# A named function table set ahead of the joined mLSTM work, and another spread of the top-k search steps over the phases of a layer

## The reference, cut to what matters

```python
# first block: the keys and queries of the forgetting attention are normalised over each head
q = rms_norm(q, gq) * (Dh ** -0.5);  k = rms_norm(k, gk)
# second kind of layer, one of four mixers (DSA): the best quarter of the keys by an index score
score = jnp.einsum('bqh,bqhs->bqs', wi, relu(q_idx @ k_idx))
score = jnp.where(k_pos <= q_pos, score, NEG_INF)
_, idx = lax.top_k(score, 128)      # then softmax attention over the chosen keys alone
```

## Time and profile before

| | us |
|---|---|
| median of 3 runs (3570.53 to 3570.90) | 3570.84 |
| the profiled execution | 3576.43 |
| its span, first to last instruction | 3574.2 |
| PE busy | 3366.0 (94%) |
| DVE busy | 1521.3 (43%) |
| ACT busy | 1306.0 (37%) |
| mean granted clock of TensorE, of full | 0.962 |

### The profile page before, as it was taken

How to read it: one execution, slowest core, us unless ns; L and a number is a source line. 1 busy time by engine, 2 the same in 40 slices (tenths; PEclk the granted TensorE clock), 3 DMA queues, 4 the chain that set the end, 5 groups by cost and what they waited for, 6 DMA issues and landing times. The chain is left out here.

```text
span 3574.2 us, 37539 instructions
## 1 busy us (share of the span) xinstructions
PE 3366.0 (94%) x14912; PEld 2676.5 (75%) x14912; DVE 1521.3 (43%) x2423; ACT 1306.0 (37%) x2224; POOL 322.1 (9%) x148
## 2 busy tenths in 40 slices
PE   7988789999999999999888999999999998889998
PEld 6755568877888888876676788878887766668886
DVE  4143431125333333344776633343334378663334
ACT  3344542223222323233366423232223335743222
POOL 0411214430000000002200000000000230000000
PEclk9998979999999999999999999999999999999999
DMA  3300213322333333332100233323333210023332
GB/s 133 100 30 24 65 36 105 96 89 84 100 94 100 95 100 95 96 102 83 42 1 24 83 99 96 95 84 99 96 98 104 89 53 7 13 66 100 95 100 71
DMA packets 77069, 280.60 MB, mean 79 GB/s; under 512 B 8800, under 2 KB 9056, under 8 KB 76640
## 3 DMA queue, kind: packets, MB, share of 16 engines
q1 hardware_dynamic: 76896, 278.21, 25.5%
HBM read 276.08 MB, written 2.10 MB: 78 GB/s over the span
## 5 line engine op out<-in xcount | busy, mean ns | idle before, releaser
L521 ACT ACTIVATE w_hi<-raw_slabs 128x1024 fp32r<-128x1024 f32 x496 | 524.3, 1057 | 1321.6 <-PE ps L561 1180.0
L536 DVE TENSOR_TENSOR w_lo<-raw_slabs,w_hi 128x1024 fp32r<-128x1024 f32 x372 | 455.1, 1224 | 748.9 <-ACT w_hi L521 748.8
L561 PE MATMUL ps<-in_hi,w_hi 128*128 128x512 f32 x1904 | 744.6, 391 | 8.3 <-DVE in_lo L878 8.2
L561 PE MATMUL ps<-in_lo,w_hi 128*128 128x512 f32 x1904 | 741.8, 390 | 0.0
L561 PE MATMUL ps<-in_hi,w_lo 128*128 128x512 f32 x1904 | 741.8, 390 | 0.0
L561 PE MATMUL ps<-parts,w_hi 128*128 128x512 f32 x2304 | 713.2, 391 | 7.7 <-PEq L385 7.7
L536 POOL TENSOR_TENSOR w_lo<-raw_slabs,w_hi 128x1024 fp32r<-128x1024 f32 x124 | 306.4, 2473 | 2623.2 <-ACT w_hi L521 2623.2
L561 PEld LDWEIGHTS ps<-parts,w_hi 128*128 128x128 f32 x2304 | 433.7, 188 | 100.0 <-issue 10.0
L561 PE MATMUL ps<-parts,w_lo 128*128 128x512 f32 x1152 | 449.2, 390 | 0.0
L561 PEld LDWEIGHTS ps<-in_hi,w_hi 128*128 128x128 f32 x1904 | 357.9, 188 | 89.3 <-issue 8.9
L561 PEld LDWEIGHTS ps<-in_lo,w_hi 128*128 128x128 f32 x1904 | 358.2, 188 | 74.4 <-issue 0.7
(11 more groups left out here) (277 smaller groups left out, 3499.6 us busy)
## 6 DMA issues: line engine op xcount, KB each, us to landing
raw_slabs<-weights SPq DMA_DIRECT2D x510, 512.0 KB, 3.6
big<-rope SPq DMA_DIRECT2D x2, 2304.0 KB, 8.8
x_resid<-xT SPq DMA_DIRECT2D x8, 256.0 KB, 4.3
outT<-x_resid SPq DMA_DIRECT2D x8, 256.0 KB, 2.0
const_cols<-consts SPq DMA_DIRECT2D x1, 836.0 KB, 8.8
scratch<-brow SPq DMA_DIRECT2D x1, 768.0 KB, 9.4
vector_cols<-vec SPq DMA_DIRECT2D x2, 45.5 KB, 9.2
vector_cols<-vec SPq DMA_DIRECT2D x1, 69.0 KB, 3.3
```

The source lines that it names most:

```text
L521: self.nc.scalar.activation(self.w_hi[:, m % SPLIT, :], self.raw[:, n % RAW, :], ACT.Copy)\
L536: (self.nc.gpsimd if i is None else self.nc.vector).tensor_tensor(self.w_lo[:, m % SPLIT, :], self.raw[:, n % RAW, :], self.w_hi[:, m % SP ...
L561: mm = k.nc.tensor.matmul(out, lhsT, rhs, start=(c == 0 and m == 0), stop=(last and m == 2))
```

## The change

A set is named once, ahead of the first exponential of the mLSTM helper. The search steps stop at 27, 32 and 44 in place of 28, 38 and 48, so that four steps, and the mask of the third block, fall into stick-breaking. In the projections one step more stands behind job 13, two more behind job 18 and two behind job 19; those behind jobs 20, 22, 24, 26, 27 and 28 are gone.

```diff
@@ -53,7 +53,7 @@
 TOPK = T // 4
 IDX_HEADS = 8
 TOP_STEPS = TOPK // 8
-TOP_CUTS = (28, 38, 48)
+TOP_CUTS = (27, 32, 44)
 INDEX_AT = (None, 35, 36, 39)
@@ -1642,6 +1642,7 @@
     def scalar(self, act, j):
         k, nc, s = self.k, self.k.nc, self.s
         if j < 0:
+            k.use_table(EXP_LN)
             nc.scalar.activation(self.em[0:4], self.em[0:4], ACT.Exp, scale=-1.0).then_inc(s["stabil"], 1)
             act.wait_ge(s["u_turned"], self.at("u_turned", 1))
@@ -2414,7 +2415,7 @@
     FIRST, EACH = 5, 3
     CMP, KV = 3, 7
-    STEPS = {**{j: 2 for j in range(8, 19)}, 20: 1, 22: 1, 24: 1, 26: 1, 27: 1, 28: 1}
+    STEPS = {**{j: 2 for j in range(8, 18)}, 13: 3, 18: 4, 19: 2}
```

## The result

| | before | after |
|---|---|---|
| median, us | 3570.69 (4 runs, 3568.99 to 3570.90) | 3540.96 (4 runs, 3531.83 to 3542.33) |
| the profiled execution | 3576.43 | 3542.33 |
| its span | 3574.2 | 3540.1 |
| mean granted clock of TensorE | 0.962 | 0.965 |

The ratio is 0.9912, 95% interval [0.9895, 0.9930]; by the medians the changed kernel is 29.7 us faster, by the ratio 31.4. The forecast was 3546.4, in a range of 3535 to 3559.

The account below looks back on a forecast made before the run. TensorE, busy in 94% of the span, was taken as the bound. Table set 19.0 us (12.7 idle, 6.3 clock) plus search steps 5.4 made 24.4 off the median 3570.84: 3546.4, range 3535 to 3559 (forecast's own 3541 to 3552).

Parts of the forecast that it names:

- Part 1, idle terms: Joined mLSTM phase: 16 table loads go; six PE waits and the last Exp's load shrink by 12.7 us in all.
- Part 1, the clock: mLSTM phase: of 8.4 us lost to half clock, three quarters come back, 6.3 us.
- Rival B: mLSTM phase: the clock does not come back, the table set gives only 12.7; 18.1 us in all, 3553; chance 0.10.
- D: mLSTM phase: loads are placed again at each Ln and Exp, only 5.4 us remain, 3565; chance 0.07.
- Part 2, projections: End of each layer's projections: less DVE backlog shortens PE's 7.45 us wait by 4.0 us, low end 1.2.
- The floor of 6.3: Projections: the most the wait ahead of the first attention could shrink, 6.3 us, set by where ACT ends.
- Part 2, first attention: First attention: DVE has 7.5 us less work, 3.0 us gained per layer, between 2.4 and 4.2; half clock left as is.
- rival C: Projections end at ACT's end and the first attention starts at full clock: 34.2 us in all, 3537; chance 0.12.
- Part 2, second attention: Second attention: two search steps more on DVE, 0.8 us lost per layer, between 0.4 and 2.5.
- Part 2, stick-breaking: Stick-breaking: four added steps, partly covered by DVE's idle times, lose 3.5 us per layer, between 1.5 and 6.3.
- rival A: Moved steps cost full price: 2.5 us lost in second attention, 6.3 in stick-breaking; 15.4 gained in all, 3555; chance 0.12.
- E: Stick-breaking: longer PE waits bring four half-clock falls of 3.25 us per layer; kernel slower, 3578; chance 0.04.

Follow-up runs that it names:

- The hidden and the unhidden loads: The changed kernel with 14 table loads put back, two in each of seven mLSTM jobs: behind the last exponential (hidden), 3533.5 us; ahead of the root's Ln, 3560.9 us.

## Why the prediction was right, and where it was not

**Part 1, idle terms: right.** The six waits went down by 1.1 (L1579), 0.9 (L1631), 1.4 (L1626 on ACT), 2.7 (L1610), 2.5 (L1626 on DVE) and 2.5 (L803), and the last one ahead of the next phase by 1.3 (3.77 to 2.49): 12.4 us for a forecast of 12.7. The hidden and the unhidden loads show that it is the place that costs. That 16 loads, 20.5 us, were worth 12.3 of idle time, is what the waits said one by one.

**Part 1, the clock: the term was too small.** 6.3 us were put down, 7.85 came. Behind its first 27 us no half clock is left in the phase (the last of the stretches at the end of this document), so all of the loss that stood there came back, not three quarters. And the estimate went by a stretch that ended at 279.7; behind it, after the wait of 4.5 us for the last sums, before had another 6.5 us at half, with PE busy for 2.0 of it, so 1.0 lost. The 8.4 us, less 1.65 for the stretch at 195.6, which both kernels have, plus that 1.0 make 7.75, for the 7.85 measured.

```profile
284.20:290.70 6.50, 2.04 (x2) 0.50 (x2) 1.50 (x2) 4.72 (x6) 0.00 (x0) 0.50 0.00 0
```

The 7.85 is one pair of profiles. PE's busy time in the phase was 99.03 and 96.92 us in the two profiles with before's loads, and 87.90 to 92.78 in the eleven that have none or have them hidden, on average 8.0 less; single pairs would give 4.1 to 11.1. Rival B, that the clock would not come back, fell. D fell with the single load.

**No drain beside a table load.** The hidden pair took 2.57 us on ACT, twice 1283 ns. The copy ahead of it ends at 197.54, and the next instruction, a cast, follows at once:

```profile
197.55 2.57 ACT L404 ACT_TABLE_LOAD   x2
200.14 1.06 ACT L521 ACTIVATE w_hi<-raw_slabs 128x1024 fp32r<-128x1024 f32 x1
```

The prediction went by the row here, and the runs bear it out.

**Part 2, projections: 4.0 said, 5.0 measured, and of its terms one was right.** The wait ahead of the first attention fell by 5.06, to 2.39. DVE starts the rotation that stands ahead of the steps of jobs 17 and 18 147.1 us into the projections in both kernels, and ends its work 179.9 us into them before and 174.8 after. What lies between can be read off in order:

- Behind that rotation came ten steps of 384 columns and now come eight. Two steps fewer are 2.5 us, where the prediction put one, 1.2; what jobs 13 and 15 take in their place lies ahead of this rotation.
- The idle time of 1.45 us is filled, as forecast.
- The instruction of line 2404 that took 1.72 us beside GpSimd's subtraction takes 0.69 at 1725.72, all of the 1.03 where 0.65 were put down. GpSimd's subtraction now runs from 1723.46 to 1725.82, and the search steps beside it keep their 0.56 and 0.54 us.
- The 0.7 us "before the last rotations" did not come: the idle time of that size, 0.75 us ahead of this same rotation, is not filled but has grown to 1.92.

These make 2.5 + 1.45 + 1.03 = 4.98 us. The floor of 6.3 was not reached either: with no step at all behind job 18, 1.5 us of wait are left, which is 5.9 off the 7.45, because DVE's last instruction there ends 0.3 us behind ACT's.

**Part 2, first attention: 3.0 said, 4.9 measured.** Two errors of one sign. DVE's five steps were worth 3.6 to 4.0, over the 3.0 taken and within its ends (2.4 to 4.2): taking DVE's lateness down by proportion was too careful. That PE's wait in each unit is the difference of two nearly equal loads, so that it shrinks faster than the load, is my reading and was not tested by itself. And the half clock behind the wait was left as it was, though part of it went with the shorter wait: 5.9 us at half (the prediction had 5) became 3.4, 1.2 us. This is the part of rival C that came true. The whole of it, 2.6 us given for a wait near 1 us, is what the kernel with seven steps in job 13 shows (27.00 against 29.46 is 2.5).

**Part 2, second attention: -0.8 said, +0.2 to +0.4 measured.** The two steps more cost nothing. PE's idle time was 4.56 with ten steps and is 3.68 with twelve, at the same clock; why twelve steps fit better than ten was not tried. The price begins behind that, and it is not one per step: 3.4 to 3.8 us more idle time at fourteen and at sixteen alike, 5.8 at seventeen.

**Part 2, stick-breaking: -3.5 said, -2.75 and -3.08 measured.** Cover by the four idle times of the earlier trace rows gave the right size, and the additions show it step by step:

```profile
1847.44 0.68 DVE L1979 SCALAR_TENSOR_TENSOR scratch<-ps,scratch 128x512 f32<-128x512 f32 x1
...
1856.93 0.68 DVE L1979 SCALAR_TENSOR_TENSOR scratch<-ps,scratch 128x512 f32<-128x512 f32 x1
...
1866.87 0.68 DVE L1979 SCALAR_TENSOR_TENSOR scratch<-ps,scratch 128x512 f32<-128x512 f32 x1
...
1876.81 0.68 DVE L1979 SCALAR_TENSOR_TENSOR scratch<-ps,scratch 128x512 f32<-128x512 f32 x1
```

Counted from the start of the phase they come 1.02, 1.38, 1.93 and 2.75 us later than before, so the four steps added 1.02, 0.36, 0.55 and 0.82 where 1.16, 0.52, 0.70 and 0.95 were forecast. The idle time ahead of each is gone. Where PE shows the delay is another matter than the prediction had it: its waits for the scan went only from 6.4 to 6.5 us, those for the copies (L1993) from nothing to 1.6. With 2.8 against 6.3 rival A fell.

E was priced far too high, but what it names does occur. In this profile the clock stayed at 1.00 in spite of waits up to 1.4 us. In six of the fourteen layers that were profiled with steps in the stick it did not: there it fell for some 3.4 us, within 1.1 us of the end of the last wait for a scan (1.4 us, the same in all fourteen). One of the six is the first layer of the changed kernel in its third profile:

```profile
1835.17:1881.11 45.94, 37.13 (x200) 27.02 (x201) 32.79 (x61) 29.86 (x81) 0.00 (x0) 0.96 0.00 1
```

None of the fourteen layers without steps there shows it. It costs 1.5 us, where E had four falls of 3.25 a layer, and in four of the six the second attention had lost 1.7 less to the clock (64.8 us for 66.5). So the sign that the prediction gave for being wrong there, a clock under 1 in stick-breaking, did show in some executions. That the wait is what brings the clock down is not shown: eight layers with the same wait kept it, and before's last wait was 1.6 us at 1.00. E's reading of the rows was off as well: the fall of 6.5 us in the mLSTM phase came behind a wait of 1.6 us, not of 2 or more.

**The sum.** 24.4 were forecast for the profiled executions, 34.1 came: the 9.7 more are 1.1 from part 1 (12.3 for 12.7 of idle time, 7.85 for 6.3 of clock), 2.2 from the projections, 3.8 from the first attentions, 2.2 from the second, 1.2 from the sticks, less 0.8 that the rest lost. By the medians it is 29.7 for 24.4. All four terms of part 2 erred on the careful side, so that their errors added up; the range held the time because it reached to rival C. The median of 3541.0 lies on the edge of the forecast's own 3541 to 3552 and nearer to rival C's 3537 than to 3546.4. Within the projections' term two errors, a step too few and an idle time that was not filled, largely cancelled; that 4.0 came so near is in part luck.

## What to carry to other kernels

Price a removed stall by what of it ends PE's waits, wait by wait, and then look at the granted clock behind each of these waits: it made 7.85 of 20.1 us in one phase here and 1.2 of 4.9 in another. Work for an engine that is not the bound is free only where its idle time lies: seven steps in one job of the projections cost PE nothing, while two more in the second attention, beyond the twelve that fit, cost it over 3 us of idle time, and the next two nothing more. A step that is moved pays only if it leaves the stretch in which its engine has no idle time: count the steps behind the last idle time, before and after. Where one kernel's runs spread over 10 us, compare phases at an equal clock; two medians of five runs do not tell 4 us.

## What was not expected of the hardware

**Which stretches run at half clock differs from execution to execution.** In the changed kernel's first profile two of some 3.3 us stand at the beginning of the mLSTM phase, with PE busy throughout, and none behind them:

```profile
174.90:178.20 3.30, 3.30 (x10) 2.53 (x9) 0.81 (x2) 0.95 (x3) 0.93 (x1) 0.51 0.90 288
195.60:198.90 3.30, 3.30 (x6) 1.65 (x5) 1.26 (x5) 1.15 (x2) 0.00 (x0) 0.51 0.00 0
198.90:271.00 72.10, 66.94 (x249) 44.07 (x247) 40.67 (x53) 31.39 (x52) 14.40 (x6) 1.00 0.10 30
```

With PE's idle time at 7.5 us each time, the same phase took 95.42 us with neither of them (no step in the stick), 97.1 with one (three profiles), 98.7 to 98.8 with both, and 100.31 in another execution of the changed kernel: differences of some 1.65 us, what one such stretch loses. Within one execution the same instructions took 175.16 us in the first layer's projections and 171.98 in the second's, with PE's idle time equal to 0.01 us (7.58 and 7.57):

```profile
1563.96:1739.12 175.16, 167.58 (x659) 118.19 (x659) 93.91 (x170) 62.23 (x99) 55.34 (x29) 0.95 0.23 75
2744.66:2916.64 171.98, 164.41 (x658) 115.90 (x659) 93.95 (x170) 62.23 (x99) 55.46 (x29) 0.97 0.24 76
```

The forgetting attention, which begins at half clock in all fourteen profiles, took 50.3 to 50.5 us in ten of them, with 23 to 24 us at half, and 54.7 to 55.0 in the other four, with some 33. What decides whether such a stretch comes is open. The changed kernel's runs spread from 3530.9 to 3542.3 us, and those of the kernel before from 3561 to 3577. The granted clock goes with this spread, if not strictly: its mean was 0.969 to 0.972 in the five fastest runs of the changed kernel and 0.965 to 0.969 in the five slowest. Whether it is the whole of the spread is not shown.

**In these profiles, the shorter the wait ahead of the first attention, the less half clock behind it.** Behind a wait of 7.3 to 7.7 us the first attention began at half clock in all profiles that had it; behind one of 1.8 to 2.6 us it began at half clock or fell to it within 1.2 us, and took 28.4 to 28.6 us, some 1.6 over full clock; behind 1.5 us it ran at full clock in seven of eight layers (27.00 or less), and in one it fell as well (26.97 where the other layer took 25.35).
